# Turned activations of the gate-and-up stage: their 16-piece swap issued by SyncE between weight loads instead of by GpSimd

## What is computed

```python
def swiglu(x, w_gu, w_down):
    g, u = jnp.split(x @ w_gu, 2, axis=-1)
    return (jax.nn.silu(g) * u) @ w_down

h = h + 0.5 * rmsnorm(swiglu(rmsnorm(h, n_ffn1_pre), w_ffn1_gu, w_ffn1_down), n_ffn1_post)
...
h = h + 0.5 * rmsnorm(swiglu(rmsnorm(h, n_ffn2_pre), w_ffn2_gu, w_ffn2_down), n_ffn2_post)
```

## Time and profile before

| | |
|---|---|
| median of 3 runs | 2433.98 us (2432.99 to 2436.94) |
| profiled execution, time | 2433.06 us |
| its span, first to last instruction | 2431.3 us |
| granted TensorE clock, mean | 0.999 of full |
| PE busy | 2410.6 us (99%) |
| DVE busy | 1840.5 us (76%) |
| ACT busy | 1336.8 us (55%) |
| POOL busy | 440.0 us (18%), 867 instructions |
| DMA | 498.53 MB, mean 205 GB/s |

### The profile page before, as it was taken

One profiled execution on the slowest core, in us unless ns is written; L12 is line 12 of the kernel. 1 busy time (PEld: TensorE's weight loads), 2 busy tenths in 40 slices (PEclk: granted clock), 3 DMA queues, 4 the chain that ended last, 5 costly groups with the idle time before them and its releaser, 6 DMA issues.

```text
span 2431.3 us, 32326 instructions
## 1 busy us (share of the span) xinstructions
PE 2410.6 (99%) x10933; PEld 1998.5 (82%) x10933; DVE 1840.5 (76%) x2219; ACT 1336.8 (55%) x1613; POOL 440.0 (18%) x867
## 2 busy tenths in 40 slices
PE   8999999999999999999999999999999999999998
PEld 7888888888888888888888888888888888888886
DVE  6999999987566456677676464465689999998885
ACT  6555555554555556657575444444655555555553
POOL 5211212201222003223242020010112121121000
PEclk9999999999999999999999999999999999999999
DMA  7777767767778765555665677676667777676665
GB/s 243 213 215 214 221 207 218 213 208 223 226 240 257 199 188 157 170 160 159 170 183 159 200 208 195 211 238 191 209 207 220 211 215 217 208 223 211 197 204 193
DMA packets 306063, 498.53 MB, mean 205 GB/s; under 512 B 28460, under 2 KB 102320, under 8 KB 305200
## 3 DMA queue, kind: packets, MB, share of 16 engines
q1 hardware_dynamic: 282336, 457.85, 62.7%
q0 software_dynamic: 23344, 38.95, 5.0%
q10 hardware_dynamic: 288, 0.52, 0.1%
HBM read 471.39 MB, written 8.52 MB: 197 GB/s over the span
## 4 chain that ended last, share of the span: by engine, by line
PE 92%; POOL 2%; DMA 2%; DVE 2%; SPq 1%; issue 1%; ACT 0%; DVEq 0%; POOLq 0%; ACTq 0%
PE acc L770 40%; PE acc L858 39%; PE mix L858 9%; POOL mkh L733 1%; DMA sq<-mk_scratch 1%; POOL mkh L730 1%; PE acc L795 1%; DMA post_a<-n_ffn_post 1%; SPq L438 0%; SPq L472 0%; PE mix L1082 0%; DVE wlo L1971 0%; PE acc L813 0%; PE mix L831 0%; PE mix L1128 0%
## 5 line engine op out<-in xcount | busy, mean ns | idle before, releaser
L1289 ACT ACTIVATE whi<-raw 128x1024 fp32r<-128x1024 f32 x860 | 902.3, 1056 | 972.4 <-PE acc L770 480.0
L1823 DVE TENSOR_TENSOR wlo<-raw,whi 128x1024 fp32r<-128x1024 f32 x568 | 687.3, 1228 | 322.8 <-ACT whi L1289 312.2
L1971 DVE TENSOR_TENSOR wlo<-raw,whi 128x2048 fp32r<-128x2048 f32 x146 | 333.6, 2285 | 54.1 <-ACT whi L1289 54.1
L770 PE MATMUL acc<-whi,u_hi 128*128 128x512 f32 x896 | 356.9, 398 | 0.0
L770 PE MATMUL acc<-whi,u_lo 128*128 128x512 f32 x896 | 349.4, 390 | 0.0
L770 PE MATMUL acc<-wlo,u_hi 128*128 128x512 f32 x896 | 349.1, 390 | 0.0
L387 POOL DMA_DIRECT2D nat<-nat x416 | 203.5, 498 | 791.9 <-DVE nat L2058 649.0
L858 PE MATMUL acc<-whi,x_hi 128*128 128x512 f32 x860 | 334.7, 389 | 0.3 <-DVE nat L1926 0.3
L858 PE MATMUL acc<-wlo,x_hi 128*128 128x512 f32 x860 | 334.6, 389 | 0.0
L858 PE MATMUL acc<-whi,x_lo 128*128 128x512 f32 x860 | 334.6, 389 | 0.0
L770 PEld LDWEIGHTS acc<-whi,u_lo 128*128 128x128 f32 x896 | 168.2, 188 | 35.8
(11 more groups left out here) (476 smaller groups left out, 3848.7 us busy)
## 6 DMA issues: line engine op xcount, KB each, us to landing
raw<-w_ffn_gu SPq DMA_DIRECT2D x352, 512.0 KB
raw<-w_ffn_down SPq DMA_DIRECT2D x176, 512.0 KB
raw<-w_in SPq DMA_DIRECT2D x224, 256.0 KB
raw<-w_in SPq DMA_DIRECT2D x96, 512.0 KB
raw<-w_mem_kv SPq DMA_DIRECT2D x32, 512.0 KB
raw<-w_out SPq DMA_DIRECT2D x32, 512.0 KB
nat<-nat POOLq DMA_DIRECT2D x416, 32.0 KB, 3.5
raw<-w_in SPq DMA_DIRECT2D x64, 128.0 KB
```

What stands on the lines that cost most here:

```text
L770: ins = nc.tensor.matmul(acc[:, par, t, :], x[:, k0 + k, cols], w[:, k, :], start=first and k == 0 and m == 0, stop=last and k == UK - 1 a ...
L1289: act(whi[:, l % RING], raw[:, l], ACT.Copy).then_inc(hi_ready, 1)
L1823: tt(wlo[:, l], raw[:, l], whi[:, l % RING].bitcast(fp32), ALU.subtract).then_inc(lo_ready, 1)
L1971: tt(wlo[:, g:g + 2], raw[:, g:g + 2], whi[:, g % RING:g % RING + 2].bitcast(fp32), ALU.subtract).then_inc(lo_ready, 2)
```

## The change

`swap_quarters` takes the issuing engine as an argument. `swap_act` now waits and issues on SP. Its calls leave GpSimd's program and stand in SP's: in each of the chunks 1 to 10 behind the load of unit 13 (SWAP_AT), and for the last chunk behind the load of unit 9 of the down projection (LAST_SWAP_AT). The other swaps (memory rows, mixer outputs, mixture) stay with GpSimd.

```diff
+SWAP_AT, LAST_SWAP_AT = 13, 9
...
-        def swap_quarters(dst, src, done):
+        def swap_quarters(dst, src, done, eng=None):
 
             for j in range(4):
                 for q in range(4):
-                    nc.gpsimd.dma_start(dst[32 * j:32 * j + 32, q * 256:(q + 1) * 256],
+                    (eng or nc.gpsimd).dma_start(dst[32 * j:32 * j + 32, q * 256:(q + 1) * 256],
                                         src[32 * q:32 * q + 32, j * 256:(j + 1) * 256]).then_inc(done, 16)
 
         def swap_act(n):
 
-            nc.gpsimd.wait_ge(sem("act_turned"), n + 1)
-            nc.gpsimd.wait_ge(sem("act_lo"), n + 1)
-            swap_quarters(swapped, turned, sem("act_swapped"))
+            nc.sync.wait_ge(sem("act_turned"), n + 1)
+            nc.sync.wait_ge(sem("act_lo"), n + 1)
+            swap_quarters(swapped, turned, sem("act_swapped"), nc.sync)
...
                         load(at(UB[f"gu{f + 1}"], i, 2 * U_D, j), j,
                              [w_gu[f][kp][:, :, ds(i * CW + c * D_FF, CW)]])
+                        if j == SWAP_AT and not isinstance(i, int):
+                            swap_act(f * N_GU - 1 + i)
...
                         load(at(UB[f"down{f + 1}"], i, 2 * U_F, j), i * 2 * U_F + j,
                              [w_dn[f][kp][:, :, ds(i * (2 * CW) + c * CW, CW)]])
+                        if i == 0 and j == LAST_SWAP_AT:
+                            swap_act((f + 1) * N_GU - 1)
...
             pl.engine_nop().then_inc(sem("act_lo"), 1)
-            for n in range(N_GU):
-                swap_act(n)
...
-            for n in range(N_GU, 2 * N_GU):
-                swap_act(n)
```

## The result

| | before | with the change |
|---|---|---|
| median | 2433.98 us (2432.99 to 2436.94, 5 runs) | 2443.10 us (2439.72 to 2445.84, 5 runs) |
| profiled execution | 2433.06 us, span 2431.3 | 2440.98 us, span 2439.3 |

The ratio is 1.0037, 95% interval 1.0023 to 1.0050: slower by 9.1 us, where I had forecast no change. The median lies 3 us above the upper end of my range.

What follows compares the result with a forecast made beforehand. PE was taken to bound the kernel, busy 99% of the span; removing POOL's issues, adding them to SP and moving the bytes each cost 0, so 2434.0 us on the median's scale, range 2430 to 2440 us.

Steps and rivals of the forecast that it cites:

- Rival 3: Whole kernel: a gain from POOL losing this work, bounded by PE's idle time at 0.35 us, 2433.6 us; chance 0.05.
- Rival 2: SP's queue: weights wait behind pieces costing 0.65 us to issue and 5.4 to land; 34 us, 2468 us; chance 0.05.
- One sign of being wrong that I had named: In the chunks: ACT waiting on `raw` in front of units 14 and 15, with PE holes once in each chunk.
- 16 x 0.46 = 7.4 us (ends: 6.3 and 10.4): SP in a chunk: time to issue a swap's 16 pieces, 0.46 us each, leaving SP free at 288.6 us.
- Cost in the chunks: 0 at both ends: Chunks: weight loads delayed by the issues still land before ACT wants them, so 0 us at middle and upper issue times.
- Each further load of a series costs 1.5 us more: Weight loads behind the swap: the first lands 3.3 us after its issue, each further one 1.5 us later.
- the edge of 491.0: Down projection: SP must be free by 491.0 us, 0.70 us a piece, or unit 11 comes late for PE.
- the spare was 1.05 us: Down projection: DVE pair ends at 498.19, PE starts on it at 499.24, so 1.05 us of lateness costs 0.
- rival 1: SP's issues at full-queue pace, 1.22 us a piece: weights late in chunks and down projections, 171 us, 2605 us; chance 0.04.
- The margins are 1.0, 0.5, 1.0 and 0.9 us: Chunk, upper issue time: how far the four loads behind the swap land ahead of ACT's high parts.
- the edge at 0.74 us a piece: Chunk: issue time per piece above which unit 15 lands too late for PE's use of the pair 14 and 15.
- Removed from POOL ... Worth: 0: POOL: 352 of 416 issues, 172 us of busy time, leave; they lie beside a PE that never stops, so 0 us.

Runs made afterwards that it cites:

- e5: Kernel before, but GpSimd issues 15 of each swap's 16 pieces and SP waits until all 15 have landed, then issues the last; 2437.27 us, ratio 1.0017.
- e3: The change with pieces spread on SP: 6, 5 and 5 behind three weight loads, in the down projection four parts of 4; 2435.06 us, ratio 1.0009.
- e6: The change with four of SP's pieces cut in two, 20 issues in place of 16, same bytes; 2501.44 us, ratio 1.0277.
- e9: e3 plus 176 idle copies between scratch rows in DRAM, issued by GpSimd in FFN 2; 2432.59 us, ratio 0.9999.
- e10: e3 plus 88 idle copies issued by GpSimd in FFN 2, 8 at each turn; 2435.15 us, ratio 1.0011.
- e11: e3 plus 176 engine nops on GpSimd in FFN 2, no copies; 2434.43 us, ratio 1.0006.
- e12: e3 plus 16 idle copies issued by GpSimd at the last turn of FFN 2 only; 2435.64 us, ratio 1.0016.
- e4: Kernel before, but GpSimd issues 15 of 16 pieces and SP waits until 12 have landed, then issues one; 2432.18 us, ratio 1.0001.
- e7: The change with each swap split, 8 pieces issued by SP and 8 by GpSimd, starting together; 2437.03 us, ratio 1.0015.

## Why the prediction was wrong

**What held.** POOL lost its 172 us and nobody gained by it. The series starts when the turn ends, and behind the load of unit 13. Rival 3's bound stands: TensorE had nothing to win. Rival 2, weights behind pieces in SP's queue, needed pieces that take 5.4 us to land; they took 1.8 in the median. The Trainium skill (DMA: Bandwidth & Descriptors, section Queues, rings and completion order) has the DMAs of one issuer consumed in order on each DMA engine. Nothing here tells for or against it: with pieces that land in 1.8 us, a load that waits for them and one that doesn't arrive alike, and e5's loads come as late behind one piece as the change's behind 16. One sign of being wrong that I had named came: ACT waited on `raw` in front of units 14 and 15, for 0.21 and 0.22 us in the chunk above. But no hole of PE came from these two.

**"16 x 0.46 = 7.4 us (ends: 6.3 and 10.4)".** The term was mis-sized: it is 10.02 us, 0.63 us a piece. The choice for the row at 0.46 was wrong and that at 0.65 nearly right. By itself this would have been harmless to my sum, since I claimed "Cost in the chunks: 0 at both ends".

**"Each further load of a series costs 1.5 us more", from a first one at 3.3 us.** Mis-sized too. From 293.54, when SP is free, ACT is held by the first load until 297.55 (4.0 us), by the second until 298.84 (5.3) and by the third until 301.39 (7.9). I had 3.3, 4.8 and 6.2 us. In the down projection I had 4.8 us for unit 11; ACT got it at 499.16, 6.0 us after 493.20. This decides there: SP is free at 493.20 less PE's lag of 2.5 us (501.52 against 499.01, the matmul ahead of 499.24) = 490.7, still ahead of the edge of 491.0 that I had worked out for rival 1. With 6.0 us unit 11 comes at 496.7, 2.0 us behind ACT's 494.74; the spare was 1.05 us, so PE loses 0.9, and 0.92 is what it lost.

**"The margins are 1.0, 0.5, 1.0 and 0.9 us. Cost in the chunks: 0 at both ends".** This step failed for the chunks (10 of the 26 matmuls), as the landing times did for the down projections. For units 14 and 15 I followed the margin to PE and found the edge at 0.74 us a piece. For the next two I stopped at ACT. Nothing on DVE was followed behind their pair, and there stands `combine`, whose end frees the sums that PE starts its next chunk on. It ended 1.1 us before PE wanted it, and with the loads 1.3 us late it came 1.2 us later. So the edge of the chunks is that of the third and fourth load, not of the second. e3, e5 and e6 show from three sides that it is the hold: same pieces without it, 0 us; a hold with one piece, 4.3 us, most of it in the two chunks where the hold was longest; 2.5 us more hold, 58 us, of which up to 14 are the clock's.

**"Removed from POOL ... Worth: 0".** Also failed, by 2.3 us. I looked for work of POOL that would start earlier and did not ask what its taking away does at the end of the program. e9 against e3, e10, e11 and e12 shows that the drain goes with GpSimd's DMAs in the last block; why it does, these runs leave open. It is not in proportion to their count: 0 give 8.5 us, 16 give 9.8, 88 give 9.75, 160 to 176 give 3.5 to 4.8. Nor is the count all of it: e4 and e5 have 165 each and drain for 4.5 and 3.9 us.

**Rival 1's mechanism was the right one** (SP held so long that PE waits for units behind it), but I let it decide from 0.70 us a piece on, for the wrong pair, and only priced it at 1.22 us. With the numbers above, the third load of the chunk may reach ACT 1.1 us late (1.3 less the 0.24 lost), so SP must be free by 298.78 + 1.1 - 7.9 = 292.0, which is (292.0 - 281.16) / 16 = 0.68 us a piece, and only 0.63 where the turn is 0.8 us late. In the down projection it must be free by 494.74 + 1.05 - 6.0 = 489.8, (489.8 - 479.8) / 16 = 0.62 us, and the turn was 0.8 us late there too. A piece takes 0.63 us, and the upper end of my own bounds was 0.65: past the second edge, and near the first. It should have made the forecast's upper end, not a rival with 0.04.

## What to carry to other kernels

Moving DMA issues to a queue that "only waits" costs what stands behind them in that queue: take the length of the hold from the upper bound of the issue time, and follow every load behind it, not the first two, through all that its consumers do next, until a step that frees something for the bounding engine. If such a series has to stand among loads, spread it: parts of at most six between loads cost TensorE nothing here, nor did 8 in a row (e7), where 16 in a row did. And when work leaves GpSimd, look at the end of the program as well as at the place it left.

## What the hardware showed that I had not expected

- GpSimd's DRAIN at the end took 3.5 to 9.8 us, and went with the DMAs that it issued in the last stage, not in proportion; up to 3.6 us of it lengthened the kernel.
- A 32 KB piece cost SP 0.63 us to issue and GpSimd 0.49 us; the queue with no busy time in the profile is the slower one.
- How fast a piece lands hangs on the other traffic, whoever issues it: 3.4 us in the median with GpSimd issuing beside the weights and 1.7 with GpSimd issuing while SP is held (e4, e5); 2.4 with SP issuing between the weights (e3) and 1.8 with SP issuing all 16 in a row (the change).
- Gaps of PE cost more than their length in e6: eight times the granted clock was 0.50 for a stretch behind them, up to 13.6 us together. The change's own gaps, 5.9 us in all, brought no such stretch.
- A late matmul is drawn as a longer one: in the changed kernel PE's busy time in two windows fell by 3.2 us, the count of its matmuls by 5.9 us' worth.
